# Four edits at once in a two-block transformer kernel: router product by column, squares summed on GpSimd, gathers with a bounds check, latents made in earlier steps, copies ahead of exponentials

## The reference, cut to what matters

```python
q = rms_norm_2(rms_norm_2(q_lat, q_a_norm) @ w_q_b)      # 4 heads of 128 + 64 rotated
kv = rms_norm_2(kv_lat, kv_a_norm) @ w_kv_b              # keys 128, values 128 a head
o = softmax(mask(qh @ kh.T)) @ vh                        # causal, per block of 128 queries
mixed = concat([rms_norm_2(attn), rms_norm_2(lru)])      # 512 + 512 columns
x = x + gate1 * (mixed @ w_out)
h2 = rms_norm_2(x, norm2_g) * (1 + scale2) + shift2
g_idx = top1(softmax(h2 @ w_rg + b_rg))                  # 4 groups
e_idx = top2(softmax((h2 @ w_re + b_re)[group]))         # 2 of its 8 experts
# rows sorted by expert, each expert padded to blocks of MOE_BLOCK = 128 rows
hid = silu(xb @ w_gate[e]) * (xb @ w_up[e])              # 1024 -> 256
x = x + gate2 * scatter_add(row_w * (hid @ w_down[e]))   # 256 -> 1024
```

## Time and profile before

| | |
|---|---|
| median of 3 runs | 3761.67 us (3759.36 to 3768.54) |
| the profiled execution | 3749.46 us, its span 3747.6 us |
| TensorE busy | 3513.6 us, 94% |
| VectorE busy | 1692.7 us, 45% |
| ScalarE busy | 1037.1 us, 28% |
| GpSimd busy | 988.4 us, 26% |
| mean granted TensorE clock | 0.975 of full speed |
| expert weights | 48 DMAs of 3072 KB, 11.9 us each to land |

### The profile page before, as it was taken

The page is one execution under the profiler, slowest core; times in us unless marked ns, Lnnn a source line. Parts: engine busy times, 40 slices in busy tenths (PEclk is TensorE's granted clock), DMA queues, the critical chain, the costliest instruction groups (busy, mean ns, idle before and its releaser), DMA issues. The chain is left out here.

```text
span 3747.6 us, 33237 instructions
## 1 busy us (share of the span) xinstructions
PE 3513.6 (94%) x11453; PEld 1838.4 (49%) x11453; DVE 1692.7 (45%) x4081; ACT 1037.1 (28%) x2543; POOL 988.4 (26%) x1362
## 2 busy tenths in 40 slices
PE   4999999999999999999999989999989978999997
PEld 3754455555445544444444445555555544444443
DVE  4666433343354763346665557443444452221221
ACT  3122222211100550012244446433322222222221
POOL 0277777500000780000000006555520001112111
PEclk7999999999999999999999989999999988999999
DMA  3134445434253103232211000001012226999997
GB/s 137 58 128 147 164 147 167 152 99 134 91 179 130 35 24 129 84 122 69 94 42 35 12 11 1 1 1 68 1 58 96 74 93 250 323 329 333 332 326 234
DMA packets 115563, 459.96 MB, mean 123 GB/s; under 512 B 13587, under 2 KB 41107, under 8 KB 103356
## 3 DMA queue, kind: packets, MB, share of 16 engines
q1 hardware_dynamic: 91484, 370.18, 27.9%
q0 software_dynamic: 18432, 67.12, 6.4%
q10 hardware_dynamic: 5472, 20.45, 1.5%
HBM read 340.28 MB, written 117.42 MB: 122 GB/s over the span
## 5 line engine op out<-in xcount | busy, mean ns | idle before, releaser
L142 PE MATMUL pst<-arena 128*128 128x512 f32 (+5 forms) x6938 | 2754.0, 555 | 68.0 <-DVE arena L158 34.1
L142 PEld LDWEIGHTS pst<-arena 128*128 128x128 f32 x6938 | 1300.0, 198 | 1399.2 <-issue 1244.3
L164 POOL TENSOR_TENSOR arena<-arena 128x4 f32<-128x4 f32 (+7 forms) x784 | 412.7, 526 | 465.3 <-DVE arena L2043 404.9
L164 DVE TENSOR_TENSOR arena<-arena 128x1 f32<-128x1 f32 (+8 forms) x1260 | 445.4, 354 | 95.3 <-ACT arena L2273 20.2
L147 PE MATMUL pst<-arena 128*128 128x128 f32 x2145 | 322.2, 289 | 119.6 <-DVE arena L246 52.5
L147 PEld LDWEIGHTS pst<-arena 128*128 128x128 f32 x2145 | 257.0, 147 | 276.9 <-issue 148.3
L1286 POOL TENSOR_SCALAR arena<-arena 128x384 f32<-128x384 f32 (+1 forms) x128 | 151.7, 1213 | 523.8 <-DVE arena L1278 522.6
L153 ACT ACTIVATE arena<-pst,arena 128x128 f32<-128x128 f32 (+1 forms) x630 | 244.8, 485 | 112.7 <-PE pst L147 112.7
L2220 POOL TENSOR_SCALAR arena<-arena 128x512 f32<-128x512 f32 (+3 forms) x160 | 219.1, 1393 | 172.5 <-DVE arena L164 158.4
L167 DVE TENSOR_SCALAR arena<-arena 128x1 f32<-128x1 f32 (+11 forms) x581 | 141.2, 243 | 180.7 <-DMA arena<-in_bc 69.1
L173 ACT ACTIVATE arena<-arena 128x1024 f32<-128x1024 f32 x48 | 50.7, 1057 | 599.2 <-DVE arena L1538 342.1
(11 more groups left out here) (194 smaller groups left out, 2105.1 us busy)
## 6 DMA issues: line engine op xcount, KB each, us to landing
arena<-in_w_exp SPq DMA_DIRECT2D x48, 3072.0 KB, 11.9
arena<-in_w_ada SPq DMA_DIRECT2D x48, 512.0 KB, 4.9
rotd<-arena POOLq DMA_DIRECT2D x32, 512.0 KB, 4.0
arena<-rotd SPq DMA_DIRECT2D x32, 512.0 KB, 4.9
arena<-sgd SPq DMA_DIRECT2D x16, 1024.0 KB, 6.8
arena<-pwd SPq DMA_DIRECT2D x32, 416.0 KB, 5.7
pwd<-arena SPq DMA_DIRECT2D x16, 576.0 KB, 5.2
h2d<-arena SPq DMA_DIRECT2D x17, 512.0 KB, 2.9
```

Source lines behind the costliest of these rows:

```text
L142: x = t.do.matmul(o, l, r, start=(i == 0), stop=(i == len(pairs) - 1))
L164: own(v, s).tensor_tensor(o, a, b, op).then_inc(*inc(s, *event))
```

## The change

Four edits, made together.

1. Latents: the tables LAT_STEP and TURN_STEP say in which step a latent tile and a turn are made. Steps 1, 5 and 9 make two tiles and steps 13 to 15 none; turns 10 and 11 stand in step 15. Projection, copies and squares of tile 0 of the next stage move into step 16, on all three engines, and tile 0 waits only for its own latents. The lr stores are waited for at V tile 12 instead of tiles 0 to 2.
2. Attention: ScalarE holds a score's exponentials back until the next item. If that is an even turn that does not need them, its copy comes first.
3. Router: xn's turned tiles are kept for four token tiles (xnT4). The router's weights are the stationary side (36 columns), 512 tokens stream past; even k write to partitions 0 to 35, odd k to 64 to 99 of the same bank. ScalarE copies both to LT, four transposes bring tokens back to rows, VectorE adds the halves and the bias. It is done once for four tiles, an iteration or two later than before. The sum of squares: ScalarE squares, GpSimd adds four 128-column pieces to one (sq1), TensorE multiplies with ones once and not four times; for the first group these products stand between the two halves of tile 0.
4. Experts: the gather gets bounds_check = S - 1 without an error, so an index at S or above is not read. TensorE's `hidden(b-1)` and VectorE's copy of it come ahead of `up(b)`.

```diff
+        LAT_STEP = [0, 1, 1, 2, 3, 4, 5, 5, 6, 7, 8, 9, 9, 10, 11, 12]
+        TURN_STEP = [4, 5, 6, 7, 8, 9, 11, 12, 13, 14, 15, 15]
...
-                if n < LJ:
-                    te_ll_lat(t, n)
+                for i in lat_tiles(n):
+                    te_ll_lat(t, i)
                 for x in lat_turns(n):
                     te_ll_turn(t, x)
+                if n == LJ:
+                    te_qk_project(t, 0)
 
...
+                if n == LJ:
+                    for x in lat_turns(n - 1):
+                        if x % 2 == 0:
+                            any_ll_turn(a, x)
                 if n >= 1:
...
+                if n == LJ:
+                    ac_qk_squares(a, 0)
...
-                if n and n % 4 == 0:
-                    ve_ll_norm(v, n // 4 - 1)
+                if n == LJ:
+                    for x in lat_turns(n - 1):
+                        if x % 2:
+                            any_ll_turn(v, x)
+                    ve_qk_evac(v, 0)
+                for j in range(4):
+                    if n == LAT_STEP[4 * j + 3] + 1:
+                        ve_ll_norm(v, j)
                 if n >= 1:
                     ve_ll_decay(v, n - 1)
                 if n < LJ:
                     ve_ll_conv(v, n)
+                else:
+                    ve_qk_evac_kv(v, 0)
                 if n >= 1:
                     ve_ll_scan(v, n - 1)
...
-            lat_done(t)
+            for m in range(3):
+                t.wait_ge(*lat_evac(i // 4 * 3 + m))
...
-            if i < 3:
-                v.wait_ge(*at(f"st_lr{(LJ - 3 + i) % 3}", "lr", LJ - 3 + i))
+            if i == 12:
+                for n in range(LJ - 3, LJ):
+                    v.wait_ge(*at(f"st_lr{n % 3}", "lr", n))
...
+            held = []
             for kind, n in ORDER:
                 if kind == "score":
-                    ac_mla_score(a, n)
+                    for m in held:
+                        ac_mla_score(a, m)
+                    held = [n]
                 else:
-                    if n % 2 == 0:
+                    own_scores = SCORE_AT[2 * TURNS[n][0] + 1, chunks_of(2 * TURNS[n][0] + 1) - 1]
+                    late = bool(held) and held[0] > own_scores
+                    if n % 2 == 0 and late:
+                        any_mla_turn(a, n)
+                    for m in held:
+                        ac_mla_score(a, m)
+                    held = []
+                    if n % 2 == 0 and not late:
                         any_mla_turn(a, n)
...
-                t.wait_ge(*at("o2_ac", "sq", i))
-                x = mm(t, bank(7)[:, i:i + 1], [(sqb[i % 4][:, k, :], ones[:, 0:1]) for k in range(4)])
+                t.wait_ge(*at("o2_po", "sq", i))
+                x = t.do.matmul(bank(7)[:, i:i + 1], sq1[i % 4], ones[:, 0:1], start=True, stop=True)
             x.then_inc(*inc("o2_pe", "sums", b))
+
+        def te_o2_logits(t, b):
+
+            t.wait_ge(*at("o2_ac", "xnT", 4 * b + 3, 1))
+            t.wait_ge(*at("ld_par", "b_rt"))
+            t.wait_ge(*at("o2_ve", "lg", b - 1))
+            for k in range(8):
+                o = t.do.matmul(bank(6)[64 * (k % 2):64 * (k % 2) + 36, :], wr[:, k, :], xnT4[k // 4][:, k % 4, :],
+                                start=(k < 2), stop=(k >= 6))
+            o.then_inc(*inc("o2_pe", "logits", b))
+
+        def te_o2_logits_turn(t, b):
+            t.wait_ge(*at("o2_ac", "LT", b))
+            trs(t, [(bank(6)[:, u * 128:(u + 1) * 128], LT[:, u * 128:(u + 1) * 128]) for u in range(4)]
+                ).then_inc(*inc("o2_pe", "lg", b))

+        def ac_o2_logits(a, b):
+            q = "o2_ac"
+            a.wait_ge(*at("o2_pe", "logits", b))
+            a.wait_ge(*at("rt_po", "made"))
+            a.wait_ge(*at("o2_pe", "lg", b - 1))
+            acopy(a, LT[0:36, :], bank(6)[0:36, :]).then_inc(*inc(q))
+            acopy(a, LT[64:100, :], bank(6)[64:100, :]).then_inc(*inc(q, "LT", b))
+
+        def ve_o2_logits(v, b):
+            q = "o2_ve"
+            b6, o = bank(6).rearrange("p (a n) -> p a n", a=4), lg[:, 4 * b:4 * b + 4, :]
+            v.wait_ge(*at("o2_pe", "lg", b))
+            v.wait_ge(*at("ld_par", "b_rt"))
+            tt(v, q, o, b6[:, :, 0:36], bc(brb, 1, [128, 4, 36]), ADD)
+            tt(v, q, o, o, b6[:, :, 64:100], ADD, "lg", b)
...
+                    if i == 0:
+                        te_o2_sums(t, 0)
...
+                if i in (5, 9, 13, 17):
+                    te_o2_logits(t, i // 4 - 1)
+                if i in (6, 10, 14, 18):
+                    te_o2_logits_turn(t, i // 4 - 1)
...
+        def po_o2(p):
+
+            q = "o2_po"
+            for i in range(NT):
+                p.wait_ge(*at("o2_ac", "sq", i))
+                p.wait_ge(*at("o2_pe", "sums", i // 4 - 1))
+                s4, o = sqb[i % 2], sq1[i % 4]
+                p.do.tensor_tensor(s4[:, 0:2, :], s4[:, 0:2, :], s4[:, 2:4, :], ADD).then_inc(*inc(q))
+                own(p, q).tensor_tensor(o, s4[:, 0, :], s4[:, 1, :], ADD).then_inc(*inc(q, "sq", i))
...
-                                    in_offset=bass.IndirectOffsetOnAxis(ap=idT[:, b:b + 1], axis=0)
+                                    in_offset=bass.IndirectOffsetOnAxis(ap=idT[:, b:b + 1], axis=0),
+                                    bounds_check=S - 1, oob_is_err=False
                                     ).then_inc(*dma(f"moe_xr{b % 3}", "xr", b))
...
             for b in range(lo, hi + 1):
+                if b > lo:
+                    te_moe_hidden(t, b - 1)
                 if b < hi:
                     te_moe_up(t, b)
-                if b > lo:
-                    te_moe_hidden(t, b - 1)
                 if b + 1 < hi:
...
         def ve_moe_run(v, lo, hi):
             for b in range(lo, hi + 1):
+                if b > lo:
+                    ve_moe_hidden(v, b - 1)
                 if b < hi:
                     ve_moe_up(v, b)
```

More of the change, by code:

```diff
@@ L1699, in lat_evac, with lat_tiles @@
             return at("ll_ve" if x % 2 else "ll_ac", "T", x)
+        LAT_STEP = [0, 1, 1, 2, 3, 4, 5, 5, 6, 7, 8, 9, 9, 10, 11, 12]
+        TURN_STEP = [4, 5, 6, 7, 8, 9, 11, 12, 13, 14, 15, 15]
+        def lat_tiles(n):
+            return [i for i in range(NT) if LAT_STEP[i] == n]
         def lat_turns(n):
-            if n == LJ:
-                return [9, 10, 11]
-            return [3 * ((n - 5) // 4) + (n - 5) % 4] if n >= 5 and (n - 5) % 4 < 3 and n < LJ else []
+            return [x for x in range(12) if TURN_STEP[x] == n]
         def te_ll_turn(t, x):
@@ L1782, in ac_ll @@
                 for x in lat_turns(n - 1):
-                    if x % 2 == 0:
+                    if x % 2 == 0 and n < LJ:
                         any_ll_turn(a, x)
@@ L1927, in ve_ll @@
                 for x in lat_turns(n - 1):
-                    if x % 2:
+                    if x % 2 and n < LJ:
                         any_ll_turn(v, x)
@@ L1938, in ve_ll @@
                     own(v, q).memset(epsc, EPS).then_inc(*inc(q, "eps"))
-                if n in (6, 10, 14, 16):
-                    ve_ll_rope(v, min(n // 4 - 1 if n < 16 else 3, 3))
-                if n < LJ:
-                    b = bank(4 + n % 2)
-                    v.wait_ge(*at("ll_pe", "raw", n))
-                    if n >= 8:
-                        v.wait_ge(*at("ll_pe", "T", 3 * (n // 4 - 2) + 2))
-                    own(v, q).tensor_copy(LAT[:, n % 8, :], b[:, 0:384]).then_inc(*inc(q))
-                    v.do.tensor_copy(KR[:, n, :], b[:, 384:448]).then_inc(*inc(q, "raw", n))
-            for x in lat_turns(LJ):
-                if x % 2:
-                    any_ll_turn(v, x)
+                if n in (6, 7, 11, 14):
+                    ve_ll_rope(v, (6, 7, 11, 14).index(n))
+                for i in lat_tiles(n):
+                    b = bank(4 + i % 2)
+                    v.wait_ge(*at("ll_pe", "raw", i))
+                    if i >= 8:
+                        v.wait_ge(*at("ll_pe", "T", 3 * (i // 4 - 2) + 2))
+                    own(v, q).tensor_copy(LAT[:, i % 8, :], b[:, 0:384]).then_inc(*inc(q))
+                    v.do.tensor_copy(KR[:, i, :], b[:, 384:448]).then_inc(*inc(q, "raw", i))
         def ve_ll_sums(v):
@@ L2057, in ve_qk @@
             for i in range(NT + 2):
-                if i < NT:
+                if 0 < i < NT:
                     ve_qk_evac(v, i)
@@ L2418, in build @@
         xn = [reg(168 + 4 * i, 1024) for i in range(2)]
-        xnT = [reg(120 + 4 * i, 8, 128) for i in range(2)]
+        xnT4 = [reg(120, 4, 512), reg(56, 4, 512)]
+        LT = reg(118, 512)
+        sq1 = [reg(188 + 0.5 * i, 128) for i in range(4)]
         wr = reg(184, 8, 36)
@@ L2422, in build @@
         lg = reg(185.5, 16, 36)
-        junk4 = reg(188, 1024)
-        sqb = [reg(48 + 2 * i, 4, 128) for i in range(4)]
+        sqb = [reg(48 + 2 * i, 4, 128) for i in range(2)]
+        junk5 = reg(52, 1024)
         orr, oss = cols[:, 64:80], cols[:, 48:64]
@@ L2497, in ve_o2 @@
             ve_o2_sums(v, 0)
```

(2 more changed lines are left out.)

94 lines of the change are left out of this document (42 added, 52 removed).

## The result

The changed kernel takes 3670.97 us (median of 4 runs, 3665.33 to 3676.62); the kernel before, on the same chip, 3760.52. The ratio is 0.9754, 95% interval 0.9731 to 0.9778. Forecast: 3664 in 3638 to 3705.

A forecast was written before the change was run, and what follows sets the result against it. TensorE was taken as the engine to shorten, with the DMA engines a near-equal bound in the expert stage. Terms -15, -19, -33 and -31 sum to -98, giving 3664 us for the median, range 3638 to 3705.

The forecast's parts named there:

- Part 1: Recurrence's end to the latent projections: latents made sooner let projection 0 follow the last sums directly; -15 us (-8 to -18.5).
- the products are only moved: steps 13 to 15 lose theirs: Recurrence: 16 instructions, some 6 us each, leave steps 13 to 15 for steps 1, 5 and 9; TensorE stays the bound.
- Part 2: Latent attention: ScalarE's copies ahead of exponentials end TensorE's 20.0 us of waits in 24 places; -19 us (0 to -22).
- rival C: Hole before the projections refilled by ScalarE's late squares, attention's stalls by GpSimd; 3684 us, chance 0.10.
- Part 3: Second output projection: router by column and squares added by GpSimd; -33 us (-12 to -37).
- the tail: After the output projection's last product: last logits wait for ScalarE's copies and run at half clock; +5 us.
- Sums and start: Output projection: fewer column-sum instructions, -10.5 us, and TensorE's wait for the first evacuation gone, -4.9 us.
- Logits: Router in the output projection: column halves run side by side, 4.5 us a group plus turns 0.45; -8 us.
- The clock: Output projection: four half-clock stretches, 34 us together, disappear with fewer small instructions in a row; -14.7 us (0 to -14.7).
- Part 4: Expert stage: gathers skip padding and the hidden turn comes earlier; block pitch 12.76 to 12.1 us, -31 us (-5 to -45).
- Rival B: Expert gather: skipped rows cost as much as read ones, pitch near 12.5 us; 3683 us, chance 0.13.
- Rival D: Expert stage: the checked gather takes GpSimd long per row; at 16 us the kernel takes 3949 us; chance 0.03.

The follow-up runs named there:

- the first of the unchecked kernels: The changed kernel with the gather's bounds check removed, so padding is read, the experts' new order kept: 3681.57 us, ratio 0.9771 to the kernel before.

## Why the prediction was right, step by step

**The sum.** Forecast -98 on the profiled time: -15, -19, -33, -31. Measured for each part alone: -9.4, -21.8, -32.8, -30.1, together -94; for the whole -89.6 by the medians on one chip. The median came 7 us above the forecast, most of it part 1. Each part took away the wait or the work that it was to take away; the bound that is left in part 4 is another than forecast. That the sum fits so well owes something to luck in parts 3 and 4, where terms that were off cancel each other.

**Part 1, a third too large.** That projection 0 follows the last sums held. The step that failed is "the products are only moved: steps 13 to 15 lose theirs", with TensorE as the only bound of a shorter step. The steps got turns in the products' place, all in bank 6, and without a product between them and the next step they meet the copy of the turn before: 4.7 us of waits. Turns in other banks gave the time back. Another 2.0 us are the turns themselves, of which twelve instructions more now stand ahead of the last sums, so that these start 6.7 us later than before (2227.4 with the offset taken off, 2220.63 before); the forecast left them where they were. The first k turn came at 2241.7, not 2237, because VectorE's evacuations of q wait for a projection that starts that much later. The 2237 was too early as a sum, too: its own terms, 2227.07 + 1.1 + 6.7 + 1.4 + 1.1 + 1.9, give 2239.3. The 2 us set aside for a clock at half speed were needed: the projection of tile 2, 12 instructions, took 6.41 us, where tiles 0 and 1 have 24 in 8.84.

**Part 2, 3 us too small.** I counted the waits of the one kind (20.0) less a margin; the whole came and 2.5 us more that I can't name, and the bound on the far side, GpSimd's rows, did not appear (4.4 us of waits for VectorE in all). So neither half of rival C came.

**Part 3, right in sum, not in each term.** The stage took 257.5 us and not 251, the tail gave back 1.1 us and not 5: the two errors cancel. Sums and start went as forecast (-10.5, -4.9). Logits: I took 4.5 us a group from the 64-row half of a score; it is 3.56, 3 us more for three groups. The Trainium skill, page "TensorEngine Tiling (Array Packing)", section Theoretical Speedup, gives up to 2x for such halves. One half and two halves give 6.99 and 3.56 here, which agrees. The nearest row misled me by its shortness. Its instructions start in pairs 7 ns apart as well; it has two pairs, each with an end of the group beside it, and takes 0.53 us a pair from start to start, where inside a group of eight pairs the step is 0.43 and only the first and the last are longer (0.46 and 0.53).

The clock: -14.7 forecast, about 1.7 left in this profile and 3.4 to 5.1 in five of the others. The forecast had the drops entered after one-column instructions, transposes and 36-column products in a row; they begin at the end of the one-column instructions, in 13 places of 16 before that place's first 36-column one, and at the first place there is none at all ahead. Against the gain stand 5.6 us of new waits for VectorE, which I had not priced, and each of the short drops that are left follows one of them: I gave cover to GpSimd's adds and never added up VectorE's tile, in which the logits' adds, the picking and the root of the next sums now follow each other. With these values the terms of the stage add up to 33.8 us, where 32.3 were measured. The tail cost 1.1 and not 5, since the logits ran at full clock; that too is chance. Three profiles of this router have a tail of 24.2 us, and in the others with the same tail it is 25.7 to 26.6, with the logits in part at half clock (5.47 us in the first of the unchecked kernels).

**Part 4, right in sum, the check's share too large.** Pitch 12.12, forecast 12.1. The forecast's working does not give that number: 11.7 us of DMA time a block is 12.3 at the share then reached, (64.7 + 30.6)%, and the term would be -22. The measured pitch went with a share of 0.97. So the right pitch was luck. Of the 0.64 us, the order alone gives 0.3 to 0.5 (12.76 to 12.88 against 12.34 to 12.45) and the check, behind it, the other 0.3, as far as the 0.3 to 0.4 us by which executions differ lets one say; the forecast's 0.43 a block took the DMA engines' total as the bound, but a load's run is (argued above), and the gather is mostly outside it. Rival B priced the new order with reads of the padding at 3683; the two runs of that kernel took 3682 and 3684. It was the right price for the wrong kernel: skipped rows do keep their packets, but small ones, and they cost next to nothing. Rival D's slow gather did not come: 1043 ns.

**Ratio of effect to noise.** The note that the profiled execution lay 12 us under the median, and was "small against both", hid a stretch of unchanged code that varies by 20 us between executions.

## What to carry to other kernels

Before two profiles are compared, find the last instruction of code that both share and take its offset off. When work is moved out of a step, look at what then stands next to each other in one bank or behind one engine; here a second and third PSUM bank took 4.7 us of waits away. When the price of a pattern is taken from a short group, look at the starts of its instructions one by one: its ends may cost more than its inside. And a high share of DMA time does not make the DMA's total the bound: compare the time from issue to landing of the one transfer that is waited for with the time that the schedule leaves it.

## What the runs showed of the hardware

- Two f32 products with 36 stationary columns on partitions 0 and 64 of one bank overlap in full: 16 instructions of 512 columns in 3.56 us, 6.99 on one half.
- An indirect gather with a bound keeps a packet for each skipped row (18432 in all, as before), of 4 bytes; its instruction takes 1043 ns against 989. Skipping 2048 of 6144 rows went with 0.3 us less a block where TensorE waited for loads, about what one execution differs from another, and with nothing where it waited for VectorE. Skipping nearly all rows gave no more.
- While a 3 MB load runs beside scatters and gathers, all 16 DMA engines are busy: 8.3 us of its own packets and 1.9 us of others between its first packet and its last.
- In the output projection the clock went to half for 6.8 to 10.2 us in four places with the old router, each within 1.9 us of the last of 32 one-column instructions (16 of 16 in four profiles), and for 3.4 us in three places with these 32 instructions and the new router. With 8 one-column instructions it went to half for 3.4 us (once 6.8) in one or two places, each 2 to 4 us after TensorE began to wait for VectorE, and nowhere in the stage in the one profile without these waits.
